# A hybrid encoder block: mixing's turn moved between two halves, attention's constant rows by fills, convolution moved ahead

## The reference, cut to what matters

```
h   = RMSNorm(x);  P = h @ W_in            # lru_x | lru_gate | q | k | v | forget
A   = RG-LRU scan(causal conv4(lru_x)) * gelu(lru_gate)
B   = softmax(q k^T / sqrt(d) + F_t - F_s) v, causal, 8 heads of 64
x   = x + concat(RMSNorm(A), RMSNorm(B)) @ W_out
h2  = RMSNorm(x)
x   = x + PEER(h2)                          # 8 heads pick 16 of 16384 one-neuron experts
out = RMSNorm(x)
```

## Time and profile before

| what | us |
|---|---|
| median of 3 runs | 3052.64 (3042.54 to 3055.24) |
| the profiled execution | 3044.79 |
| its span | 3043.0 |
| of it `recur` | 131 to 300 |
| `attend` | 300 to 522 |
| `mix_out` | 522 to 686 |

### The profile page before, as it was taken

The page is one execution under the profiler, slowest core; times in us unless marked ns, Lnnn a source line. Parts: engine busy times, 40 slices in busy tenths (PEclk is TensorE's granted clock), DMA queues, the critical chain, the costliest instruction groups (busy, mean ns, idle before and its releaser), DMA issues. The chain is left out here.

```text
span 3043.0 us, 40193 instructions
## 1 busy us (share of the span) xinstructions
PE 2759.7 (91%) x15003; PEld 2410.1 (79%) x15003; DVE 2355.4 (77%) x4166; ACT 1256.3 (41%) x2507; POOL 1435.0 (47%) x1118
## 2 busy tenths in 40 slices
PE   7998799879998889999999999991999999999996
PEld 6776566339998889999999999981887877878885
DVE  3375586234976999798898978866999999999997
ACT  3244333012222247878877778841222222222222
POOL 1121310002855585555545555533666666666763
PEclk9999798989999999999999999995999999999998
DMA  4110100212103489999989899979999999999996
GB/s 115 42 35 25 45 1 21 69 42 56 32 26 100 157 291 328 351 341 345 356 319 368 319 352 362 359 301 350 385 376 372 380 373 375 376 376 383 386 386 238
DMA packets 315442, 754.28 MB, mean 248 GB/s; under 512 B 22944, under 2 KB 141728, under 8 KB 312688
## 3 DMA queue, kind: packets, MB, share of 16 engines
q0 software_dynamic: 111104, 403.02, 35.6%
q1 hardware_dynamic: 203088, 344.50, 32.0%
q10 hardware_dynamic: 1056, 4.19, 0.3%
HBM read 659.35 MB, written 92.27 MB: 247 GB/s over the span
## 5 line engine op out<-in xcount | busy, mean ns | idle before, releaser
L1815 POOL DMA_INDIRECT v_rows<-in_peer_v,row_numbers x384 | 597.8, 1557 | 381.8 <-DVE y L1879 257.2
L1608 POOL DMA_INDIRECT u_rows<-in_peer_u,row_numbers x384 | 539.4, 1405 | 433.9 <-DVE row_weights L1712 376.7
L1510 PE MATMUL expert_pre<-h2T,uT_hi 128*128 128x320 f32 x4096 | 679.3, 315 | 59.0 <-DVE uT_lo L1695 30.8
L1510 PEld LDWEIGHTS expert_pre<-h2T,uT_hi 128*128 128x128 f32 x4096 | 621.1, 191 | 64.2 <-DVE uT_lo L1695 34.2
L1921 PE MATMUL expert_out<-v_hi,w_hi 128*128 128x512 f32 x1280 | 502.7, 393 | 85.4 <-DVE w_lo L1858 85.3
L1879 DVE SCALAR_TENSOR_TENSOR y<-v_rows,row_weights,y 128x1024 f32<-128x1024 f32 x384 | 488.9, 1279 | 60.3 <-DMA v_rows<-in_peer_v,row_numbers 42.8
L1921 PE MATMUL expert_out<-v_lo,w_hi 128*128 128x512 f32 x1280 | 501.0, 391 | 0.0
L1921 PE MATMUL expert_out<-v_hi,w_lo 128*128 128x512 f32 x1280 | 500.7, 391 | 0.0
L1712 DVE CUSTOM_DVE_ANT_0 u_rows<-u_rows,h_rows_kept 128x1024 f32<-128x1024 f32 x384 | 464.6, 1237 | 5.5 <-DMA u_rows<-in_peer_u,row_numbers 5.5
L1921 PEld LDWEIGHTS expert_out<-v_hi,w_hi 128*128 128x128 f32 x1280 | 241.9, 189 | 142.3 <-DVE w_lo L1858 91.9
L1839 ACT ACTIVATE w_hi<-acts_times_gates 128x640 fp32r<-128x640 f32 x128 | 94.8, 741 | 604.7 <-DVE acts_times_gates L1851 604.5
(11 more groups left out here) (301 smaller groups left out, 4226.2 us busy)
## 6 DMA issues: line engine op xcount, KB each, us to landing
u_chunk<-in_peer_u_turned SPq DMA_DIRECT2D x128, 512.0 KB, 6.9
v_chunk<-in_peer_v SPq DMA_DIRECT2D x128, 512.0 KB, 9.5
acts_dram<-expert_acts SPq DMA_DIRECT2D x128, 320.0 KB, 5.0
gates_dram<-pick_memory SPq DMA_DIRECT2D x20, 2048.0 KB, 10.9
acts_times_gates<-acts_dram SPq DMA_DIRECT2D x128, 320.0 KB, 10.7
gates_group<-gates_dram SPq DMA_DIRECT2D x32, 1280.0 KB, 18.5
w_in_columns<-in_w_in SPq DMA_DIRECT2D x20, 512.0 KB, 3.9
wq_tile<-in_peer_wq SPq DMA_DIRECT2D x16, 512.0 KB, 4.1
```

Source lines behind the costliest of these rows:

```text
L1510: last = nc.tensor.matmul(pre[:, (2 * c + half) % 4, 0:WIDTH], part[:, c % 2, k], m.h2T[:, t, k, HALVES[half]], start=n == 0, stop=n == le ...
L1608: pool.indirect_dma_start(rows[:, k % RING], None, d.peer_u, bass.IndirectOffsetOnAxis(ap=m.row_of[:, f, slot:slot + 1], axis=0)).then_inc ...
L1815: pool.indirect_dma_start(rows[:, k % ROW_RING], None, d.peer_v, bass.IndirectOffsetOnAxis(ap=m.row_of[:, f, slot:slot + 1], axis=0)).then ...
```

## The change

There are three parts. In `recur` DVE's `conv(p + 1)` goes ahead of `fraction(p)` for tiles 1 and 2. In `attend` POOL's fills of the two source tiles and its nine copies are gone; DVE fills the rows of all three slots with three instructions, placed before `low(0)`, and POOL and ScalarE wait for these. In `mix_out` PE's order becomes, for each b: first half of tile b + 2, turn of tile b, second half of tile b + 2. The programs of the other engines in `mix_out` stay as they are.

```diff
@@ recur, DVE
-                for p in range(CT):
-                    fraction(p)
+                fraction(0)
+                conv(1)
+                recurrence(0)
+                for p in range(1, CT):
                     if p + 1 < CT:
                         conv(p + 1)
+                    fraction(p)
                     recurrence(p)
@@ attend
-        zeros, full = squares[:, 0], squares[:, 1]
@@ attend, POOL
-                step(pool.memset(zeros, 0.0))
-                step(pool.memset(full, 1.0))
...
-                for slot in range(SLOTS):
-                    step(pool.tensor_copy(k_more[64:P, slot], zeros[64:P]))
-                    step(pool.tensor_copy(q_more[64:P, slot], zeros[64:P]))
-                    step(pool.tensor_copy(k_more[MAX_ROWS, slot], full[MAX_ROWS]))
-                    pool.sem_inc(rows_set, 1)
+                pool.wait_ge(rows_set, 3)
@@ attend, PE
-                pe.wait_ge(masked, 16)
+                pe.wait_ge(masked, 14)
@@ attend, ACT
-                    act.wait_ge(rows_set, SLOTS)
+                    act.wait_ge(rows_set, 3)
@@ attend, DVE
+                v.memset(k_more[64:P].bitcast(F32), 0.0).then_inc(rows_set, 1)
+                v.memset(q_more[64:P].bitcast(F32), 0.0).then_inc(rows_set, 1)
+                dve.wait_ge(rows_set, 2)
+                v.memset(k_more[MAX_ROWS].bitcast(F32), 1.0).then_inc(rows_set, 1)
                 low(0)
-                dve.wait_ge(masked, 15)
+                dve.wait_ge(masked, 13)
...
-                dve.wait_ge(rows_set, SLOTS)
+                dve.wait_ge(masked, 14)
                 place_tops(0)
@@ mix_out, PE
-                def mix(b):
-                    for to, of, first, which in ((out_lru, m.gateT, 0, LRU_READ), (out_fox, m.foxT, CT, X2)):
-                        done = lru_mixed if which == LRU_READ else fox_mixed
-                        if b:
-                            pe.wait_ge(dve4, added(b - 1, which))
...
+                def mix(b, to, of, first, which, done):
+                    if b:
+                        pe.wait_ge(dve4, added(b - 1, which))
...
+                mix_lru = lambda b: mix(b, out_lru, m.gateT, 0, LRU_READ, lru_mixed)
+                mix_fox = lambda b: mix(b, out_fox, m.foxT, CT, X2, fox_mixed)
...
-                mix(0)
-                mix(1)
+                for b in range(2):
+                    mix_lru(b)
+                    mix_fox(b)
                 for b in range(NT):
                     if b + 2 < NT:
-                        mix(b + 2)
+                        mix_lru(b + 2)
                     turn(b)
+                    if b + 2 < NT:
+                        mix_fox(b + 2)
```

More of the change, by code:

```diff
@@ L1042, in _ @@
                 pe.wait_ge(m.w_out_in, 16)
-                def mix(b):
-                    for to, of, first, which in ((out_lru, m.gateT, 0, LRU_READ), (out_fox, m.foxT, CT, X2)):
-                        done = lru_mixed if which == LRU_READ else fox_mixed
-                        if b:
-                            pe.wait_ge(dve4, added(b - 1, which))
[L1049 to L1053, removed]
+                def mix(b, to, of, first, which, done):
+                    if b:
+                        pe.wait_ge(dve4, added(b - 1, which))
+                    for half, cols in enumerate(halves(2)):
+                        for c in range(CT):
+                            last = nc.tensor.matmul(to[:, half], of[:, c, b * P:(b + 1) * P], w[:, first + c, cols],
+                                                    start=c == 0, stop=c == CT - 1)
+                    last.then_inc(done, 1)
+                mix_lru = lambda b: mix(b, out_lru, m.gateT, 0, LRU_READ, lru_mixed)
+                mix_fox = lambda b: mix(b, out_fox, m.foxT, CT, X2, fox_mixed)
                 def turn(b):
```

## The result

The changed kernel takes 3009.48 us (median of 6 runs, 3003.56 to 3019.21), against 3049.80 for the kernel before in its own six (3042.54 to 3055.24). The ratio is 0.9874, with a 95% interval of 0.9852 to 0.9896. The forecast was 3010.5 in a range of 2999 to 3023, and faster with a chance of 0.93. The profiled execution has a span of 3006.7 us, 36.3 under the one before. The same kernel measured again, beside seven other runs of the kernel before, gave 0.9874 (0.9856 to 0.9892).

What follows compares the result with a forecast made beforehand. Early stages were taken to be bound by chains between engines (mixing, POOL's queue at attention's start), shifting all that follows; 32.7 + 5.5 + 0 = 38.2 us off 3048.7 gives 3010.5, range 2999 to 3023.

Steps and rivals of the forecast that it cites:

- Mixing: Mixing stage: PE's turn between the two halves takes DVE's chain out of its way, 32.7 us gained.
- The period: Mixing, tile to tile on PE: two halves of 6.87 and a turn of 0.79, 14.53 us against 20.33.
- The rival with late rows (4): Mixing: late rows hold turn and second half; 12.2 us later than computed in all six periods gives some 3064; chance 0.02.
- The clock: Mixing: PE resumes after each gap at its lower clock level, costing 1.8 us more per gap, within the 32.7.
- Attention's start: Start of attention: fills go from POOL to DVE, PE's row logits start at 318.4 instead of 323.88, 5.5 us gained.
- Fills: Start of attention, DVE: 3.3 us a fill, three with their waits 10.0 us, bounds 2.73 and 3.63 each.
- Subtractions and copies one after the other: Start of attention: DVE's subtractions (2.47 us) and POOL's copies (3.28) hold each other off, so they add up.
- Rival 1: Start of attention: low parts and copies don't hold each other off, fills are short; 2.4 to 4.2 us more; chance 0.22.
- rival 2: Start of attention: only handed from POOL to DVE, fills and set-up interfering; gain 1.5, some 3014.5 us; chance 0.13.
- The recurrence: Recurrence: the convolution fits into DVE's 10.28 us wait for tanh, but the root still sets the pace; worth 0.
- signs of being wrong: PE waiting on rows or the second addition inside a mixing period, a turn dearer than 1.04, or a longer expert stage.
- Rival 3: Expert stages: the time comes back there, leaving under 15 us gained, so 3035 to 3050 us; chance 0.06.

Runs made afterwards that it cites:

- low-parts run: The changed kernel with head 0's low parts ahead of DVE's three fills; single execution, PE starts 17.71 us after POOL's first instruction.
- slot 0 first: The changed kernel with DVE filling only slot 0, behind the low parts, and POOL the others after head 0's copies; ratio 0.9858, again 0.9859.

## Why the prediction was right

**Mixing.** Predicted 32.7 us, measured 32.5 (164.4 to 131.9); alone, 32.7. The period was to be 14.53 and is 14.61: the only term of it that is off is the turn, for which I took the recurrence's 0.79 and which costs 0.88. Six of these make 0.5 us, of which the stage's first half gave 0.2 back (9.04 us, 9.23 before). The last chain of 14.0 us stayed, from 630.75 to 644.75. The rows were to be 3.3 us early and are 3.4. The rival with late rows (4) had its mechanism right: with the turn moved one place further ahead it appears, at 3.39 us a time. To be slower by 0.5% it needed rows 12 us later than computed; they came as computed, 3.4 us before the turn.

**The clock** was predicted as 1.8 us for each gap. Filling the gap without removing the wait gives 1.7 a period. This part of the explanation is shown, not argued. That it is not a fixed price for a gap shows in the two periods of 18.22 us with the turn ahead of both halves.

**Attention's start.** Predicted 5.5 us, measured 6.3 in the changed kernel and in the part alone (17.2 us against 23.5). Fills: three in 10.0, measured 9.87 (301.19, where the split ends, to 311.06). Subtractions and copies one after the other: 5.8, measured 316.25 - 311.06 = 5.2. The two subtractions and POOL's first two copies took 4.16 us where their sum is 4.66, so they did overlap by some 0.5 us; which part of an instruction isn't held off is open. Rival 1 (no mutual exclusion, 2.4 to 4.2 us more) is refuted by the copies' 2.02 and 1.92 us and by the low-parts run, where the copies are short again, rival 2 (fills and POOL's set-up hold each other off) by POOL's 0.30 us beside a fill. The low-parts run also shows that the other order wins nothing: its copies are free of the exclusion, but the 2.5 us of subtractions stand ahead of the fills in full, and PE starts 0.5 us later. What brings the start forward is less on the chain, as slot 0 first does.

**The recurrence** was put at 0 and is 0, with the waits moved as described. One pair of traces would have misled: it shows the stage 1.7 us shorter.

**The sum.** 32.5 + 6.3 for the two parts gives 38.8 against 38.2 predicted. In the profiled pair 36.3 remain: the clock gave 1.7 in the recurrence, the rest of attention was 1.2 shorter (granted clock 0.91 against 0.90), the expert side took 4.9, and the stages before the recurrence 0.5. The medians of six differ by 40.3. A longer expert stage was one of my signs of being wrong, and in this pair it is there; but 4.9 us lie within the 18 us over which it varies. Rival 3 (given back later) needed under 15 us left, and is out: the mixing part alone gives its whole gain, and the expert side doesn't follow the gains. The choice of the middle of four executions as base, 3048.7, was borne out by the six runs' 3049.8. That the forecast is off by only 1 us is luck, since the six executions of the changed kernel lie 15.7 us apart.

## What to carry to other kernels

When an engine alternates between two kinds of work and the release of the one depends on the other, put the short one where its answer can travel under the long one, and work out the margin on both sides: here one place too early cost 27.5 us and one too late 32.5. Before an edit is credited with a stage's difference, run it alone: here 1.7 us of clock looked like the third part's gain. And if an instruction is moved to an idle engine, ask what it will now run beside, and whether all of it is needed for the first use.

## What was not expected of the hardware

- The record of a DVE fill is shorter than the time that the fill adds to its queue, and the rest stands as idle time in front of the record: 2.62 us for 3072 elements with fills 3.20 apart, 0.91 for 1024 with fills 1.07 apart. What follows a fill and is none starts 0.03 us after the record. The difference of the two steps is 2.13 us for 2048 elements, 1.04 ns each. That agrees with the one cycle per element that the Trainium skill states (VectorE: DVE Perf Modes, section Zero memsets can be issued as uint32 (trn2)), taken at that page's 0.96 GHz; the records' own difference, 0.83 ns, does not.
- A DVE fill and POOL's work left each other alone, while two-operand subtractions and POOL's copies took turns (2.02 and 1.92 us for copies of 1.04 and 1.03, and 0.88 us for a subtraction of 0.17). Both agree with the Trainium skill (SBUF — State Buffer, section Who interferes with whom). A DVE cast with one operand did not stay clear: of 0.17 us, it took 0.96 to 0.98 beside such a copy in three of the four profiles with slot 0 first.
- The same gap of 3.39 us in PE cost 1.7 us of clock in four of the six periods behind one and nothing in the other two. After a gap of 0.33 us the half took 7.13 us, 0.1 over the others, all five times.
